# Router and dense experts with the tokens as the stationary side, tile by tile

## The reference, cut to what matters

```
def hier_moe(x2d, w_grp, b_grp, w_exp, b_exp, w_gate, w_up, w_down):
    grp_prob = jax.nn.softmax(xf @ w_grp + b_grp, axis=-1)
    g_val, g_idx = lax.top_k(grp_prob, 1)
    exp_logits = (xf @ w_exp + b_exp).reshape(T, N_GROUPS, EXPERTS_PER_GROUP)
    sel = jnp.take_along_axis(exp_logits, g_idx[:, :, None], axis=1)[:, 0]
    e_val, e_idx = lax.top_k(jax.nn.softmax(sel, axis=-1), TOP_K_IN_GROUP)
    weights = g_val * e_val / jnp.sum(e_val, axis=-1, keepdims=True)
    ...
    for e in range(N_EXPERTS):
        h = jax.nn.silu(x2d @ w_gate[e]) * (x2d @ w_up[e])
        y = y + combine[:, e:e + 1] * (h @ w_down[e])
    return y
```

## Time and profile before

| | us |
|---|---|
| median of 3 runs | 1855.3 |
| the profiled execution's own time | 1847.47 |
| its span | 1845.7 |
| TensorE busy (matmuls) | 1785.6 (97%) |
| VectorE busy | 1204.1 (65%) |
| ScalarE busy | 941.8 (51%) |
| GpSimd busy | 106.9 (6%) |

### The profile page before, as it was taken

How to read it: one execution, slowest core, us unless ns; L and a number is a source line. 1 busy time by engine, 2 the same in 40 slices (tenths; PEclk the granted TensorE clock), 3 DMA queues, 4 the chain that set the end, 5 groups by cost and what they waited for, 6 DMA issues and landing times.

```text
span 1845.7 us, 25890 instructions
## 1 busy us (share of the span) xinstructions
PE 1785.6 (97%) x10718; PEld 1549.3 (84%) x10718; DVE 1204.1 (65%) x1512; ACT 941.8 (51%) x1243; POOL 106.9 (6%) x78
## 2 busy tenths in 40 slices
PE   7999989999999899999998999999999999999999
PEld 7999788888888788889897888888888989878887
DVE  5955478777778765558967655555545897765553
ACT  6444366555555644356754544454444666445442
POOL 1423020000000000000110000000000011000000
PEclk9999999999999999999999999999999999999999
DMA  8420155999999465545323465556554632245553
GB/s 268 129 72 1 47 172 205 336 337 332 335 333 331 141 188 189 192 160 183 92 81 108 153 188 190 193 162 203 183 186 168 194 115 69 93 158 183 183 184 113
DMA packets 181013, 329.90 MB, mean 179 GB/s; under 512 B 6688, under 2 KB 149408, under 8 KB 168096
## 3 DMA queue, kind: packets, MB, share of 16 engines
q1 hardware_dynamic: 180752, 327.73, 53.1%
q0 software_dynamic: 144, 0.52, 0.1%
HBM read 327.18 MB, written 1.05 MB: 178 GB/s over the span
## 4 chain that ended last, share of the span: by engine, by line
PE 76%; DVE 14%; ACT 4%; DMA 3%; issue 2%; POOL 0%; DVEq 0%; ACTq 0%; SPq 0%
PE ps L540 73%; DVE rlo L1495 4%; PE ps L543 3%; DVE arena L1484 3%; DMA ring<-in_few_gu 2%; ACT rhi L2292 2%; ACT arena L2292 1%; DMA ring<-in_w_in 1%; DVE arena L1487 1%; DVE arena L2137 1%; DVE small L2198 0%; DVE small L2083 0%; DVE arena L2185 0%; DVE xnl L1484 0%; DVE arena L2233 0%
## 5 line engine op out<-in xcount | busy, mean ns | idle before, releaser
L1495 DVE TENSOR_TENSOR rlo<-ring,rhi 128x2048 fp32r<-128x2048 f32 x272 | 622.5, 2291 | 334.8 <-ACT rhi L2292 334.1
L2292 ACT ACTIVATE rhi<-ring 128x2048 fp32r<-128x2048 f32 x272 | 518.0, 1908 | 256.4 <-DMA ring<-in_few_gu 122.9
L540 PE MATMUL ps<-rhi,xnh 128*128 128x512 f32 (+2 forms) x784 | 307.8, 393 | 0.0
L540 PE MATMUL ps<-rlo,xnh 128*128 128x512 f32 (+2 forms) x800 | 307.5, 384 | 0.0
L540 PE MATMUL ps<-rhi,xnl 128*128 128x512 f32 (+2 forms) x784 | 302.1, 385 | 0.0
L540 PE MATMUL ps<-xnh,rhi 128*128 128x256 f32 (+1 forms) x760 | 222.0, 292 | 3.5 <-DVE xnl L1484 2.6
L540 PE MATMUL ps<-xnl,rhi 128*128 128x256 f32 (+1 forms) x760 | 216.4, 285 | 0.0
L540 PE MATMUL ps<-xnh,rlo 128*128 128x256 f32 (+1 forms) x760 | 216.2, 285 | 0.0
L540 PE MATMUL ps<-rhi,hhi 128*128 128x512 f32 x544 | 205.9, 396 | 3.7 <-ACT arena L2292 3.7
L540 PE MATMUL ps<-rhi,xwr 128*128 128x512 f32 x528 | 180.4, 403 | 2.1 <-issue 1.8
L540 PEld LDWEIGHTS ps<-rlo,xnh 128*128 128x128 f32 x800 | 150.5, 188 | 28.5 <-issue 0.7
(11 more groups left out here) (244 smaller groups left out, 2223.1 us busy)
## 6 DMA issues: line engine op xcount, KB each, us to landing
ring<-in_few_gu SPq DMA_DIRECT2D x66, 1024.0 KB, 5.1
ring<-in_w_in SPq DMA_DIRECT2D x45, 1024.0 KB, 5.3
ring<-in_ffn_w_gate SPq DMA_DIRECT2D x88, 512.0 KB, 4.0
ring<-in_ffn_w_up SPq DMA_DIRECT2D x88, 512.0 KB, 5.0
ring<-in_ffn_w_down SPq DMA_DIRECT2D x44, 1024.0 KB, 4.9
ring<-in_exp_w_down SPq DMA_DIRECT2D x35, 1024.0 KB, 5.1
ring<-in_w_out SPq DMA_DIRECT2D x20, 1024.0 KB, 4.9
ring<-in_w_in SPq DMA_DIRECT2D x4, 896.0 KB, 4.7
```

Of the source, the lines that this page charges most:

```text
L540: return e.matmul(o, lhsT, rhs, start=start, stop=stop, skip_group_check=True)
L1495: e.tensor_tensor(lo, raw, f32(hi), SUB).then_inc(*w.hit("lo", n))
L2292: return e.activation(o, x, func, **kw)
```

## The change: what it does

- **Loads.** A dense expert's two loads hold gate and up together, four of the eight column blocks each, where one load held gate and one up (each load now comes as two transfers of 512 KB). The router's high part goes to a buffer of its own (`lat_hi`) and no longer takes one of the three slots.
- **TensorE.** The tokens are the stationary side: `router_tile(tt)` makes the logits of one tile (24 matmuls, 36 columns moving), already with the tokens on the partitions; `dense_half(x, half, tt)` sums gate and up of expert x in one bank, for one tile and four column blocks (12 matmuls of 512 columns). The products silu(gate)*up must be turned for the down product: `dense_turn(x)`, 4 transposes. `router_tile(0)` and `dense_half(0, 0, 0)` stand ahead of the turn of tile 1.
- **VectorE and ScalarE.** In `sums_and_norm` VectorE adds tile 1 after half of tile 0; the first dense load's part is made before the sums; gate and up are handled by tile (128x256), and `hi` and `lo` of the hidden values are written from the turned bank: `lo` by VectorE (`dense_lo`), where GpSimd did it (`h_lo`).

```diff
-        plan("router", I["router"].rearrange("p (c n) -> p c n", c=8))
+        plan("router", I["router"].rearrange("p (c n) -> p c n", c=8), own_hi="router")
         for x in range(ND):
-            plan(("moe", x), cols(I["exp_w_gate"][0, x], 0, 256))
-            plan(("moe", x), cols(I["exp_w_up"][0, x], 0, 256))
+            for c in (0, 4):
+                plan(("moe", x), *(cols(I[g][0, x], 0, 256)[:, c:c + 4] for g in ("exp_w_gate", "exp_w_up")))
...
+        dense_bank = lambda x, tt: ((1, 2), (3, 7))[x][tt]
+        turned_bank = (4, 3)
...
+            def router_tile(tt):
+                wh, wl_ = parts(take(ld("router")))
+                if tt == 0:
+                    bank(0, ("lg", 1))
+                for c in range(8):
+                    w.wait_ge("tile_lo", 1, tt, c // 2)
+                    p = mm3(PS[0][:, 64 * tt:64 * tt + 36], xnh[:, c, tok(tt)], xnl[:, c, tok(tt)], wh[:, c], wl_[:, c], tt + c == 0, tt * c == 7)
+                if tt:
+                    p.then_inc(*w.hit("lg_mm"))
+                    spent[ld("router")] = ("lg_mm",)
+
+            def dense_half(x, half, tt):
+                wh, wl_ = (v.rearrange("p (m c) n -> p m c n", m=2) for v in both(take(ld(("moe", x), half))))
+                b = dense_bank(x, tt)
+                if not half:
+                    bank(b, ("hf", x, tt))
+                for c in range(4):
+                    w.wait_ge("tile_lo", 1, tt, 2 * half + c // 2)
+                    p = mm3(PS[b][:, :], xnh[:, 4 * half + c, tok(tt)], xnl[:, 4 * half + c, tok(tt)], wh[:, :, c], wl_[:, :, c],
+                            half + c == 0, half * c == 3)
+                p.then_inc(*w.hit(("gate", "up")[half], x, tt))
+                spent[ld(("moe", x), half)] = (("gate", "up")[half], x, tt)
+
+            def dense_turn(x):
+                bank(turned_bank[x], ("f_lo", x))
+                for tt in range(2):
+                    w.wait_ge("hf", x, tt)
+                    for k in range(2):
+                        p = tr(PS[turned_bank[x]][:, 256 * k + 128 * tt:256 * k + 128 * tt + 128], hft[:, x, tt, 128 * k:128 * k + 128])
+                p.then_inc(*w.hit("h_T", x))
+
             def experts():
+                router_tile(0)
+                dense_half(0, 0, 0)
                 tile_turn(1, 1)
...
+                router_tile(1)
+                dense_half(0, 0, 1)
+                dense_half(0, 1, 0)
+                dense_half(0, 1, 1)
+                dense_half(1, 0, 0)
+                dense_half(1, 0, 1)
+                dense_turn(0)
                 ranks()
-                up(1, 1, ld(("moe", 1), 1), 1)
+                dense_half(1, 1, 0)
+                dense_half(1, 1, 1)
                 for x in range(ND):
                     if x == ND - 1:
+                        dense_turn(1)
                         gather()
-                    w.wait_ge("h_lo", x)
+                    w.wait_ge("f_lo", x)
                     for b in range(4):
                         bank(4 + b, ("moe", x, b))
...
-                w.wait_ge("lg_T")
+                w.wait_ge("lg_mm")
                 router()
+                part(n + 3)
+                hf_of(0)
                 part(n + 4)
-                hf_of(0, 0)
+                dense_lo(0)
                 slots()
-                hf_of(1, 1)
+                hf_of(1)
                 part(n + 5)
+                dense_lo(1)
...
-                silu_of(0, 0)
                 router()
+                silu_of(0)
                 part(n + 4)
-                silu_of(1, 1)
-                h_hi(0, 0, 0)
+                dense_hi(0)
+                silu_of(1)
                 part(n + 5)
-                h_hi(1, 1, 2)
+                dense_hi(1)
```

More of the change, by code:

```diff
@@ L1119, in experts @@
-                wh, wl_ = parts(n)
-                bank(4, ("lgT",))
-                for c in range(8):
-                    normed(1, c)
-                    p = mm3(PS[4][0:36, 0:256], wh[:, c], wl_[:, c], xnh[:, c, :], xnl[:, c, :], c == 0, c == 7)
-                p.then_inc(*w.hit("lg_mm"))
-                spent[n] = ("lg_mm",)
-                gate(0, 0, ld(("moe", 0)), 1)
-                w.wait_ge("lgT")
-                bank(5, ("lg", 1))
-                for tt in range(2):
-                    p = tr(PS[5][:, 64 * tt:64 * tt + 36], lgT[0:36, tok(tt)])
@@ L1854, in extras, with hf_of, dense_lo @@
                 e.tensor_copy(extra_expert[:, :], xfacts[:, :, 0]).then_inc(*w.hit("few_info"))
-            def hf_of(id_, i):
-                w.wait_ge("up", id_)
-                w.wait_ge("silu", id_)
-                e.tensor_tensor(hf[:, i % 2], two(2 + i % 2), sg[:, i % 2], MUL).then_inc(*w.hit("hf", id_))
+            def hf_of(x):
+                for tt in range(2):
+                    w.wait_ge("silu", x, tt)
+                    e.tensor_tensor(hft[:, x, tt], PS[dense_bank(x, tt)][:, 256:512], sgt[:, x, tt], MUL).then_inc(*w.hit("hf", x, tt))
+            def dense_lo(x):
+                w.wait_ge("h_hi", x)
+                e.tensor_tensor(hlo[:, 2 * x:2 * x + 2], two(turned_bank[x]), f32(hhi[:, 2 * x:2 * x + 2]), SUB).then_inc(*w.hit("f_lo", x))
             def window(i):
@@ L2299, in part @@
                 w.dma(d_slot[n % NR], x["landed"])
-                if x["own_hi"]:
+                if x["own_hi"] not in (None, "router"):
                     w.wait_ge("h_T", x["own_hi"])
@@ L2351, in norm_tile_of @@
                     act(tile_r[:, tt:tt + 1], tile_r[:, tt:tt + 1], ACT.Sqrt).then_inc(*w.hit("tile_std", i, tt))
+                if i == 1 and tt:
+                    part(ld(("moe", 0), 1))
                 for b in banks:
@@ L2537, in router, with silu_of, dense_hi @@
                 act(rsc[:, 44:46], rsc[:, 44:46], ACT.Exp).then_inc(*w.hit("top2_e"))
[L2539 to L2545 removed]
+            def silu_of(x):
+                for tt in range(2):
+                    w.wait_ge("up", x, tt)
+                    act(sgt[:, x, tt], PS[dense_bank(x, tt)][:, 0:256], ACT.Silu).then_inc(*w.hit("silu", x, tt))
+            def dense_hi(x):
+                w.wait_ge("h_T", x)
+                act(hhi[:, 2 * x:2 * x + 2], two(turned_bank[x]), ACT.Copy).then_inc(*w.hit("h_hi", x))
             def few_window(i):
```

42 lines of the change are left out of this document (11 added, 31 removed).

## The result

After takes 1859.05 us (median of 13 runs, 1851.86 to 1862.33), before 1852.43 in the same comparison (13 runs, 1846.0 to 1855.32). The ratio is 1.0034, 95% interval 1.0022 to 1.0046: slower by 0.34%, some 6.3 us (4.1 to 8.5). A second comparison gave 1857.74 against 1853.84, ratio 1.0017 (0.9996 to 1.0039). The time lies in the range of the prediction, but on the side that had 0.27.

What follows compares the result with a forecast made beforehand. TensorE, busy 97%, bounds the kernel; the change is worth what it moves VectorE's first-expert sum. That came 2.0 us later (+0.5 without the clock's fall), so 1855.3 + 2.0 = 1857.3 us, range 1851.6 to 1860.8.

Steps and rivals of the forecast that it cites:

- the side that had 0.27: Whole kernel slower than before by over 0.2% (3.7 us): chance 0.27, against 0.61 within 0.2% and 0.12 faster.
- To the turn of tile 1: TensorE after `w_out`: tile 0's router ends at 237.4, first dense group at 240.1, tile 1's turn at 241.0, as before.
- the clock's term: TensorE falls to half clock once, at `dense_turn(0)`: +1.7 us; ends 0 and 3.2 (a second fall, at the router).
- Rival 2: TensorE's clock also falls at the first router tile: VectorE's first-expert sum +3.3 to +5.0 us; chance 0.17 above 3.7 us.
- The narrow matmul: Router matmul of 36 columns taken as 0.102 us, ends 0.07 and 0.122; TensorE's router work +2.0 us.
- The exclusion: GpSimd's two subtractions lock out VectorE: +2.0 us ahead of a `lo` and +2.0 in `router()`.
- rival 1: No lock between GpSimd and VectorE, or GpSimd finds gaps: VectorE's first-expert sum -3.5 us, 1851.8; half, -1.5; chance 0.22.
- The wait at `dense_turn(0)`: TensorE idle 3.7 us ahead of `dense_turn(0)`, waiting for `hf` behind VectorE's `router()`; then one clock fall, +1.7.
- The bank and the order: First down product waits for `hf_of(1)` over bank 7; `dense_lo(1)` precedes VectorE's first-expert sum, at 278.5 instead of 276.50.
- The stage behind: Chosen experts' stage, 289.70 to 620, moves as a whole and hands on the 2.0 us.
- rival 3: Chosen experts' stage does not hand the shift on: a few us either way, 1853 to 1861; chance 0.13.
- The 7.8 us: Median of runs lies 7.8 us above the profiled execution; the same distance was kept for the forecast, 1849.5 to 1857.3.

Runs made afterwards that it cites:

- the mixed kernel: After, with the router's narrow matmuls spread among the wide ones of the dense group behind them, for both tiles: 1857.97 us, 1.0031 against before.
- the mixed kernel with VectorE's subtractions: The mixed kernel with both subtractions made by VectorE instead of GpSimd and ScalarE's copy of tile 0 earlier: 1848.96 us, 0.9985 against before.

## Why the prediction missed the likeliest case

**The step that failed** is the one on TensorE in "To the turn of tile 1": "so the router ends at 237.4 and the first dense group (12 x 0.228) at 240.1. ... its turn is queued behind that group. It ends at 241.0, as before", with the clock's term at one fall (+1.7) and its upper end, for two, at 3.2 us. In after the group ended 3.5 us later than that (250.83, less the 7.26 by which after's transposes of tile 0 start later than in the earlier trace rows, is 243.57), and a second fall followed in the other router tile. The term was too small as well: each of the two falls cost TensorE 3.4 us, and the one at `dense_turn(0)` in the mixed kernel 3.0 (it worked at half clock from 267.53 to 273.55). One reason is in the prediction's words "less what the narrow ones do not lose": they do lose, `ranks` took 1.99 us there (268.44 to 270.43) where 1.03 was reckoned. Rival 2 had named this mechanism, its place and its test (half clock in 234 to 241; it began at 243.9, which is 236.6 there), priced at +3.3 to +5.0. Measured in s it is +4.0 to +4.5. It was given 0.17 above 3.7 us because the clock of before was still full after 4 us of idling; of the four profiles with after's order at the router three show the fall and one doesn't, so a full clock in one execution says little about the next.

**The narrow matmul** was taken at 0.102 us with 0.122 as the end; it was 0.112. The Trainium skill's 60 cycles ("TensorE: Matmul & The Clock Gate", section "Back-to-back issue gap") are 0.025 us at 2.4 GHz; the rows do not agree.

**The exclusion** came out in place, and nearly in size: +2.0 ahead of the `lo` (1.9 measured: 4.18 against 2.29) and +2.0 in `router()` (2.5, of which some 0.9 are the memset's, which the prediction did not list). That scans wait too, which it took from the rule, is seen in the kernel with the router's weights stationary: the first TENSOR_TENSOR_SCAN of `router()` took 2.26 us beside a subtraction, where it takes 0.17 alone. Moving both subtractions away gave 6.1 us on the mixed kernel, so the term carries the wait and the fall at `dense_turn(0)` with it; rival 1 had this at 5.5 (from +2.0 to -3.5), and s of 41.83 against 44.68 is -2.9.

**The wait at `dense_turn(0)`** (3.7 us, then half clock) was not in after: TensorE was late itself. It is in the mixed kernel, 3.05 us, where all of this part of the prediction can be read, less the 6.45 us by which its tile 0 transposes start later than in the earlier trace rows: `router()` at 249.5 to 258.4 (predicted 250.2 to 258.6), `hf` done at 261.4 (261.5), the sum at 279.7 (278.5). There s is +3.2 against the earlier trace rows or +2.7 against before's second profile, with +2.0 forecast; the excess of 1.2 us is the fall's, 3.0 where 1.7 was taken.

**The bank and the order** were right: the first down product waited 1.17 us for `hf`, the sum stood behind `dense_lo(1)`. The prediction took both as given; taking them away was worth 3.1 us of s, in the mixed kernel with VectorE's subtractions.

**The stage behind** did not hand it all on. The first chosen expert's window (`xwr`) is still 4.0 us late in after against before's second profile (61.10 us behind tile 0's transposes against 57.14), but the transposes at the stage's end, with a wait of 2.19 us ahead of them, start at 622.21 against 619.20, which is 383.13 against 380.48: 2.65 us late. After's second profile has 383.01. A third of the shift was lost on the way, which is rival 3's case. The 5.1 us between the spans are made up otherwise: 0.4 arose ahead of tile 0's transposes, 2.65 came through, and another 1.6 arose between 1016 and 1071 us, where TensorE's clock falls in after (near 1024) and not in before. No run links that fall with the change.

**The 7.8 us** between execution and median, carried through as a constant, were mostly the fall at 192 us. That 1857.3 lies so near the measured 1859.05 is luck in part: the median of 3 runs from which it starts, 1855.3, is 2.9 us above that of 13 runs, 1852.43. The shift itself was forecast as 2.0 us and measured as some 6.3 (3.1 in the second comparison). And the range's ends, 1851.6 and 1860.8, are not quite those of the rivals that they are said to come from (1855.3 - 3.9 = 1851.4 and 1860.3).

What stays open: what decides whether the clock falls at the narrow matmuls in a given run, and whether this alone sets after's median. The mixed kernel speaks against the latter: with full clock at the router it is as slow as after, since the wait for VectorE and the fall behind it take the place. The two runs of after at 1847.6 us speak for it. Open is also where the stage of the chosen experts loses 1.3 us of the shift.

## What to carry to other kernels

When an instruction on one engine is made narrow or moved earlier, list what runs beside it on the engines that exclude each other, not only what waits for it: here the edit was on TensorE, and part of its cost was that GpSimd's two subtractions slid from a wait of VectorE into VectorE's work. Where two paths are nearly equal, repairing one can show almost nothing (1.3 us of s here, for a clock repair that was worth 7.1 once the other path was short); repair both before judging either, and do not share the cost out between them by one order of repairs. And compare stages from a common start, since a fall of the clock far ahead moved every later time by 7 us in some executions.

## What the runs showed of the hardware

- TensorE dropped to 1.2 GHz in a row of 24 matmuls of 36 columns, 0.5 us behind a wait of 0.65 us (at 243.9 above), and with the same instructions and waits kept 2.4 GHz in another execution. In the kernel with tile 0 behind the turn it dropped at 259.9 just behind such a row without any wait. Spread among matmuls of 512 columns, in part behind a wait of 0.80 us, they did not bring it down in any of the five profiles of such kernels.
- A matmul of 36 columns with a new stationary side in the rounded format takes 0.112 us at 2.4 GHz and 0.213 at 1.2: it goes with the clock.
- A GpSimd subtraction holds up even VectorE's smallest step: TENSOR_SCALAR on 128x2 took 2.74 us, beside the subtraction and the memset behind it, where it takes 0.17 alone, while the TENSOR_REDUCE just ahead of it, beside the same subtraction, took 0.16. The Trainium skill states both, "SBUF — State Buffer", section "Who interferes with whom": `tensor_reduce` never contends on this chip, and `tensor_tensor` with both inputs in SBUF and `tensor_scalar` can; the trace agrees.
- GpSimd's memset of 128x1024, which only writes, held a TENSOR_SCALAR (0.65 us instead of 0.17, at 261.25 above), but not a `lo` with two inputs: in the kernel with the first subtraction early that ended at 256.72, 2.1 us after the subtraction's end at 254.58, with the memset beside it up to 255.46.
